# Triangular inverse of the scan in 32x32 blocks, with the last doubling as one off-diagonal block

## The chip, the cores and the metric

The kernel runs on one core of one Trainium2 chip. The metric is the device time of one execution in microseconds; the time to compare with is the median of three runs of the kernel before.

## What is computed

One inference step of a hybrid trunk layer. The input projection feeds two kinds of heads: attention heads, and eight RWKV-7 heads of width 64 whose state runs over time in both directions. Then come an output projection and routed experts. The change touches the RWKV part alone:

```
def rwkv_scan(r, decay, k, v, kk, a, s0, reverse):
    def step(s, inp):
        r_t, w_t, k_t, v_t, kk_t, a_t = inp
        sa = jnp.einsum('bhvk,bhk->bhv', s, -kk_t)
        s = (s * w_t[:, :, None, :] + sa[..., None] * (kk_t * a_t)[:, :, None, :]
             + v_t[..., None] * k_t[:, :, None, :])
        return s, jnp.einsum('bhvk,bhk->bhv', s, r_t)
```

There are 1152 tokens: 1024 of the sample and 128 of the prompt.

## The kernel before

The stages follow one another with a barrier between them: `head` (conditioning, norm, constant masks), `rwkv`, `attention`, `output`, `topk`, `experts`, `final`.

`rwkv` does not run the recurrence token by token. Time is cut into chunks of `CH` = 64 tokens, 18 in all. Within a chunk the recurrence is a linear system with a unit triangular 64x64 matrix I + L, so a chunk needs W = (I + L)^-1, some products of 64x64 matrices, and one state handed from chunk to chunk. Heads are taken in four pairs (`p`). The two heads of a pair lie in partitions 0 to 63 and 64 to 127 (`HS`), and both directions (`d`) are worked at once. Two chunks (`i`) make a group (`g`), so a pair has 9 groups and the kernel 36. All matmuls of a group are f32; TensorE runs each as two passes, and each pass has a weight load of its own, so a matmul of the code is two MATMUL and two LDWEIGHTS records.

What a group of the code does, with the names that the text uses:

- `M_products` (L652) multiplies B and KB by Q and R of a chunk. DVE's `masked` (L1178) multiplies the 64x128 results by the triangle masks `causal` and stores them in `M`.
- `inverse_start`: DVE builds the first W from the 2x2 blocks (L1186, L1192). PE multiplies it by the identity to get its transpose T (L700), and ACT copies T into `TW` (L950).
- Five doublings, `LV` = 5. Each has `level_X` (PE, L712: M by T), `level` (DVE, L1198: mask into X), `level_Y` (PE, L723 and L727: the updates of T and of W) and `added` (DVE, L1210: add to `TW`). The last doubling leaves T out. With 64x64 blocks all of them use full 64x64 products; the mask `level` picks the blocks that count.
- The state chain of the group before runs between these: `state_Z` (L737, and L746, L751 for the output), `state_U` (L762, W by Z), `state_S` (L772, L778). Each of two chunks needs Z, U and S in turn, with DVE (L1219, L1229, L1244) and ACT (L955, L960, L961) steps between.
- `tok_major` (L672) and `PV_KV` (L685, L688) prepare products for the group's own state chain.

The order in which these stand on PE, ACT and DVE is written out by hand in a loop over `g` on each engine; the engines meet by semaphores. PE takes its instructions in order, so an instruction that waits holds all behind it. At the end of a pair stands `finish`, and the projections of the next pair follow.

Of the kernel before, what the change touches and what calls it, by code (L numbers as in the profile page):

```python
# [26 lines left out]
P = 128  # L27
# [6 lines left out]
CH = 64  # L34
CHUNKS = NT // CH
# [85 lines left out]
def head(K, A):  # L121
# [8 lines left out]
    with ctx:  # L130
# [33 lines left out]
        with nc.Block() as block:  # L164
# [96 lines left out]
            def _(dve):  # L261
# [50 lines left out]
                for h in range(2):  # L312
                    hs = slice(h * CH, (h + 1) * CH)
                    V.tensor_copy(K.idc[hs, :], K.ident[hs, hs])
                    V.tensor_copy(K.causal[hs, :, :, :], tri[hs, :, :, hs])
                for lev in range(6):
                    link(V.tensor_scalar(cmp[:, :], xorf[:, :], float(2 ** (lev + 1)), None, ALU.is_lt))
                    link(V.scalar_tensor_tensor(cmp[:, :], xorf[:, :], float(2 ** lev), cmp[:, :], ALU.is_ge, ALU.mult))
                    for d in range(2):
                        for h in range(2):  # L320
                            hs = slice(h * CH, (h + 1) * CH)
                            last = V.scalar_tensor_tensor(K.level[hs, d, lev, :], cmp[hs, hs], -1.0, low[hs, d, hs],
                                                          ALU.mult, ALU.mult)
# [43 lines left out]
def rwkv(K, A):  # L367
# [10 lines left out]
    LV = 5  # L378
# [6 lines left out]
    with ctx:  # L385
# [26 lines left out]
        TW = [sb(f"TW{i}", [P, 2, 2, 2, CH]) for i in range(2)]  # L412
        X = sb("X", [P, 2, 2, CH])
        N0 = sb("N0", [P, 2, 2, CH])
# [5 lines left out]
        HS = [slice(h * HN, (h + 1) * HN) for h in range(2)]  # L420
        bank = K.bank
# [33 lines left out]
        t0ps, t0_ok, tw_ok = sem("T0_psum"), sem("T0_ok"), sem("TW_ok")  # L455
        xps, x_ok, yps = sem("X_psum"), sem("X_ok"), sem("TW_psum")
        zps, z_ok, ups, u_ok = sem("Z_psum"), sem("Z_ok"), sem("U_psum"), sem("U_ok")
# [13 lines left out]
        with nc.Block() as block:  # L471
# [55 lines left out]
            def _(pe):  # L527
# [69 lines left out]
                for p in range(PAIRS):  # L597
# [95 lines left out]
                    def inverse_start(g):  # L693
                        pe.wait_ge(w0_ok, p * GR + g + 1)
                        for d in range(2):
                            if g:
                                pe.wait_ge(tw_ok, p * (GR * NTW) + g * NTW - 1 + d)
                            for i in range(2):
                                for hs in HS:
# [1669 lines left out]
```

## Time and profile before

| | us |
|---|---|
| median of three runs (3862.14 to 3871.79) | 3862.87 |
| the profiled execution's own time | 3860.96 |
| its span | 3859.2 |
| one group of the scan in its steady part | 15.0 |
| groups | 36 |
| granted TensorE clock, mean of the span | 0.967 |

The span runs from the first to the last instruction of the profiled execution; the execution's own time has under 2 us around it. PE is TensorE's matmul record, PEld its weight load, DVE VectorE, ACT ScalarE. A matmul's record is longer than the time for which it keeps the array from the next one, since matmuls are pipelined; a row that merges n of them shows the time from the first's start to the last's end, and the spacing is read from that.

### The profile page before, as it was taken

Reading aid. Unit: us, or ns where it says so; the run is one execution under the profiler, and the core shown is the slowest. Engines: PE = TensorE matmul, PEld = TensorE weight load, DVE = VectorE, ACT = ScalarE, POOL = GpSimd, SP = SyncE. Lnnn points to the kernel's source line nnn. Section 1 sums busy time; section 2 is a strip of 40 time slices with the busy share of each in tenths; the row PEclk is TensorE's granted clock in tenths of the full one; section 3 lists DMA queues with packets and bytes.
Section 4 is the critical chain, followed back from the end, with each engine's and each line's share of the span. In section 5 each row is a group of like instructions: output and inputs, shape, how many; then the busy total and the mean of one; then the engine's idle time right before and its main releaser. Section 6 shows DMA issues by size and latency. Waiting matters only on the chain. (4 is left out here: it accounts for less than half of the span.)

```text
span 3859.2 us, 81746 instructions
## 1 busy us (share of the span) xinstructions
PE 3562.1 (92%) x37038; PEld 3101.1 (80%) x37038; DVE 1231.4 (32%) x3103; ACT 671.1 (17%) x1677; POOL 192.0 (5%) x150
## 2 busy tenths in 40 slices
PE   5899899999899979289999999999999999999995
PEld 2387685959555545189999999999999999999995
DVE  3376767777444443701111111111111111111112
ACT  2323324242144532100000000000000000000001
POOL 0010101010000000000000000000000000000000
PEclk7899999999999999589999999999999999999997
DMA  7200000000121022098887878788787878878773
GB/s 323 61 16 10 15 5 20 4 19 4 27 79 31 18 72 94 21 354 292 274 266 263 267 259 273 261 273 268 265 267 258 273 262 269 268 268 269 258 251 110
DMA packets 498393, 664.38 MB, mean 172 GB/s; under 512 B 31183, under 2 KB 437095, under 8 KB 494975
## 3 DMA queue, kind: packets, MB, share of 16 engines
q1 hardware_dynamic: 492238, 640.23, 49.5%
q0 software_dynamic: 5632, 18.88, 1.9%
q8 instruction: 291, 4.77, 0.5%
q14 instruction: 56, 0.45, 0.0%
q10 hardware_dynamic: 176, 0.05, 0.0%
HBM read 630.70 MB, written 28.36 MB: 171 GB/s over the span
## 5 line engine op out<-in xcount | busy, mean ns | idle before, releaser
L2094 PE MATMUL bank<-e_hid,e_wd 128*128 128x144 f32 x5632 | 760.1, 288 | 0.0
L2082 PE MATMUL bank<-e_xT,e_wg 128*128 128x144 f32 x5632 | 749.5, 286 | 1.0 <-ACT e_xT L2136 1.0
L2082 PE MATMUL bank<-e_xT,e_wu 128*128 128x144 f32 x5632 | 748.1, 286 | 0.0
L2082 PEld LDWEIGHTS bank<-e_xT,e_wg 128*128 128x128 f32 x5632 | 715.5, 190 | 1.0 <-issue 1.0
L2094 PEld LDWEIGHTS bank<-e_hid,e_wd 128*128 128x128 f32 x5632 | 710.5, 190 | 5.6
L2082 PEld LDWEIGHTS bank<-e_xT,e_wu 128*128 128x128 f32 x5632 | 714.4, 190 | 0.0
L2179 DVE TENSOR_TENSOR e_tm<-bank,e_sg 128x144 f32<-128x144 f32 x352 | 108.3, 308 | 1853.0 <-ACT e_sg L2143 1853.0
L2143 ACT ACTIVATE e_sg<-bank 128x144 f32<-128x144 f32 x352 | 102.2, 290 | 1998.4 <-PE bank L2082 1998.4
L532 PE MATMUL bank<-hT_x,wblk 128*128 128x512 f32 (+1 forms) x672 | 237.5, 511 | 14.5 <-DMA wblk<-in_w_in 8.5
L532 PEld LDWEIGHTS bank<-hT_x,wblk 128*128 128x128 f32 x672 | 114.1, 197 | 130.4 <-issue 112.4
L727 PE MATMUL bank<-r_TW,r_X 64*64 64x64 f32 x2880 | 167.5, 220 | 4.3 <-DVE r_X L1198 1.3
L1210 DVE TENSOR_TENSOR r_TW<-r_TW,bank 128x256 f32<-128x256 f32 (+1 forms) x360 | 135.4, 392 | 36.8 <-PE bank L727 33.0
L723 PE MATMUL bank<-r_X,r_TW 64*64 64x64 f32 x2304 | 142.1, 218 | 2.7 <-DVE r_X L1198 2.7
L727 PEld LDWEIGHTS bank<-r_TW,r_X 64*64 64x64 f32 x2880 | 136.2, 135 | 9.3 <-DVE r_X L1198 9.3
L1462 PE MATMUL bank<-hT_x,wblk 128*128 128x512 f32 (+1 forms) x384 | 138.7, 500 | 4.5 <-PEq L89 4.5
L712 PE MATMUL bank<-r_TW,r_M 64*64 64x64 f32 x2880 | 127.4, 223 | 5.7
L1198 DVE TENSOR_TENSOR r_X<-bank,level 128x128 f32<-128x128 f32 x360 | 96.6, 290 | 83.2 <-PE bank L712 79.7
L723 PEld LDWEIGHTS bank<-r_X,r_TW 64*64 64x64 f32 x2304 | 116.7, 135 | 4.1 <-DVE r_X L1198 3.8
L712 PEld LDWEIGHTS bank<-r_TW,r_M 64*64 64x64 f32 x2880 | 103.4, 134 | 16.7 <-ACT r_TW L950 9.7
L2182 DVE TENSOR_TENSOR e_hid<-bank,e_tm 128x144 f32<-128x144 f32 x352 | 108.2, 307 | 12.2
L1462 PEld LDWEIGHTS bank<-hT_x,wblk 128*128 128x128 f32 x384 | 62.6, 193 | 52.1 <-issue 50.6
L2049 POOL DMA_INDIRECT scratch_ffn<-e_ye,idx x16 | 25.8, 1610 | 1298.6 <-DVE e_ye L2198 1298.6
(324 smaller groups left out, 3469.9 us busy)
## 6 DMA issues: line engine op xcount, KB each, us to landing
e_wg<-in_e_gate SPq DMA_DIRECT2D x176, 1024.0 KB, 5.5
e_wu<-in_e_up SPq DMA_DIRECT2D x176, 1024.0 KB, 8.1
e_wd<-in_e_down SPq DMA_DIRECT2D x176, 1024.0 KB, 11.0
h_wmod<-in_w_mod SPq DMA_DIRECT2D x24, 1024.0 KB, 17.1
wblk<-in_w_in SPq DMA_DIRECT2D x22, 512.0 KB
h_x<-in_x_sample SPq DMA_DIRECT2D x8, 512.0 KB, 6.6
wo<-in_w_out SPq DMA_DIRECT2D x2, 2048.0 KB, 11.6
o_x<-in_x_sample SPq DMA_DIRECT2D x8, 512.0 KB, 4.2
```

What stands on the lines that cost most here:

```text
L532: last = nc.tensor.matmul(bank[first + c][:, 0:n], wblk[buf][:, kc, :], K.hT[:, kc, at:at + n], start=(kc == 0), stop=(kc == KD - 1))
L712: last = nc.tensor.matmul(bank[2 + d][hs, i * CH:(i + 1) * CH], M[g % 3][hs, d, i, 0, 0:CH], TW[g % 2][hs, d, 0, i, :], start=True, stop=True)
L723: nc.tensor.matmul(bank[4 + d][hs, i * CH:(i + 1) * CH], TW[g % 2][hs, d, 1, i, :], X[hs, d, i, :], start=True, stop=True)
L727: last = nc.tensor.matmul(bank[4 + d][hs, P + i * CH:P + (i + 1) * CH], X[hs, d, i, :], TW[g % 2][hs, d, 1, i, :], start=True, stop=True)
L1198: V.tensor_tensor(X[:, d, :, :], bank[2 + d][:, 0:P].rearrange("p (i t) -> p i t", t=CH), K.level[:, d, lev, :].unsqueeze(1).broadcast_to( ...
L1210: V.tensor_tensor(TW[g % 2][:, d, a:2, :, :].rearrange("p a i t -> p (a i t)"), TW[g % 2][:, d, a:2, :, :].rearrange("p a i t -> p (a i t) ...
L1462: last = nc.tensor.matmul(piece_bank(p, n)[:, 0:m], wblk[b][:, kc, :], K.hT[:, kc, at:at + m], start=(kc == 0), stop=(kc == KD - 1))
L2082: last = nc.tensor.matmul(bank[6 + b % 2][:, j * TOK:(j + 1) * TOK], w[s][:, k, f], xT[e % 2][:, k, :], start=(k == 0), stop=(k == KD - 1))
L2094: last = nc.tensor.matmul(bank[k // PER_BANK][:, c:c + TOK], wd[s][:, b % DUO, k * P:(k + 1) * P], hid[:, b % 2, :], start=(b == 0 and k % ...
L2143: nc.scalar.activation(sg[b % 2][:, :], bank[6 + b % 2][:, 0:TOK], ACT.Sigmoid).then_inc(sg_ok, 1)
L2179: V.tensor_tensor(tm[b % 2][:, :], bank[6 + b % 2][:, 0:TOK], sg[b % 2][:, :], ALU.mult)\
L2182: V.tensor_tensor(hid[:, b % 2, :], bank[6 + b % 2][:, TOK:2 * TOK], tm[b % 2][:, :], ALU.mult)\
```

## The change

The inverse is doubled only up to 32x32 blocks: `LV` falls from 5 to 4, and `X`, `N0`, `TW`, `level` hold 32 columns instead of 64 and use each partition quarter (`QS`) for its own diagonal block. `M_products` writes the parts of B by Q as 32x32 tiles, so that each quarter of the partitions finds its diagonal block in columns 0 to 31 and its off-diagonal block in columns 32 to 63; R and KB keep their shapes. The first T of a group comes from DVE's block transpose; PE's product with the identity and ACT's two copies are gone. The last doubling is one off-diagonal block per chunk, direction and head: `last_X` and `last_Y` on PE with an ACT copy between, and ACT puts the 64x64 inverse together in `WF` by eight activations on 32 partitions. `last_X` and `last_Y` of a group stand in the next group's code. `PV_KV` moves ahead of the fourth `level_X`.

```
-    LV = 5
+    LV = 4
...
                     def M_products(g, d):
                         for i in range(2):
-                            at = piece(d, 2 * g + i)
-                            for q, src in enumerate((B[d], KB[d])):
-                                for hs in HS:
-                                    last = nc.tensor.matmul(bank[d][hs, (2 * i + q) * P:(2 * i + q + 1) * P],
-                                                            src[hs, at], QR[d][hs, :, at], start=True, stop=True)
+                            at, c = piece(d, 2 * g + i), 2 * i * P
+                            for h, hs in enumerate(HS):
+                                for b in range(2):
+                                    rows = QS[2 * h + b]
+                                    own, other = at.start + b * HB, at.start + (1 - b) * HB
+                                    nc.tensor.matmul(bank[d][rows, c:c + HB], B[d][hs, own:own + HB],
+                                                     Q[d][hs, own:own + HB], start=True, stop=True)
+                                    nc.tensor.matmul(bank[d][rows, c + HB:c + CH], B[d][hs, own:own + HB],
+                                                     Q[d][hs, other:other + HB], start=True, stop=True)
+                            for hs in HS:
+                                nc.tensor.matmul(bank[d][hs, c + CH:c + P], B[d][hs, at], R[d][hs, at],
+                                                 start=True, stop=True)
+                            for hs in HS:
+                                last = nc.tensor.matmul(bank[d][hs, c + P:c + 2 * P], KB[d][hs, at], QR[d][hs, :, at],
+                                                        start=True, stop=True)
...
                             for i in range(2):
-                                for hs in HS:
-                                    last = nc.tensor.matmul(bank[2 + d][hs, i * CH:(i + 1) * CH],
-                                                            M[g % 3][hs, d, i, 0, 0:CH], TW[g % 2][hs, d, 0, i, :],
+                                for qs in QS:
+                                    last = nc.tensor.matmul(bank[2 + d][qs, i * HB:(i + 1) * HB],
+                                                            M[g % 3][qs, d, i, 0, 0:HB], TW[g % 2][qs, d, 0, i, :],
                                                             start=True, stop=True)
...
+                    def last_X(g):
+
+                        pe.wait_ge(tw_ok, p * (GR * NTW) + (g + 1) * NTW)
+                        for i in range(2):
+                            for d in range(2):
+                                for h in range(2):
+                                    src, to = QS[2 * h + d], QS[2 * h + 1 - d]
+                                    last = nc.tensor.matmul(bank[2][to, i * HB:(i + 1) * HB],
+                                                            M[g % 3][src, d, i, 0, HB:CH], TW[g % 2][src, d, 0, i, :],
+                                                            start=True, stop=True)
+                        last.then_inc(xlps, 1)
...
+                    def last_X(g):
+                        act.wait_ge(xlps, p * GR + g + 1)
+                        nc.scalar.activation(XL[:, :, :].rearrange("p i t -> p (i t)"), bank[2][:, 0:CH], ACT.Copy,
+                                             scale=-1.0).then_inc(xl_ok, 1)
+                        for q, qs in enumerate(QS):
+                            b = q % 2
+                            nc.scalar.activation(WF[g % 2][qs, :, :, b * HB:(b + 1) * HB], TW[g % 2][qs, :, 1, :, :], ACT.Copy)
+
+                    def last_Y(g):
+                        act.wait_ge(ylps, p * GR + g + 1)
+                        for q, qs in enumerate(QS):
+                            d = q % 2
+                            last = nc.scalar.activation(WF[g % 2][qs, d, :, (1 - d) * HB:(2 - d) * HB],
+                                                        bank[5][qs, CH:P].rearrange("p (i t) -> p i t", t=HB), ACT.Copy)
+                        last.then_inc(wf_ok, 1)
...
+                        dve.wait_ge(w0_ok, p * GR + g + 1)
+                        for d in range(2):
+                            V.transpose(TW[g % 2][:, d, 0, :, :].rearrange("p i t -> p (i t)"),
+                                        TW[g % 2][:, d, 1, :, :].rearrange("p i t -> p (i t)")).then_inc(t0_ok, 1)
```

`level_Y` changes as `level_X` does (four quarters instead of two halves), and `state_U` reads `WF` instead of `TW`. The masks made in `head` are copied in more and smaller pieces.

PE's order from the end of one group to the start of the next. Names read output, then inputs; the shape is output partitions by columns. Before, the group ends with `PV_KV`, the fifth doubling (L712, L727), the next group's T (L700) and its first `level_X`:

```order
L685 MATMUL bank<-r_vtok,r_M 64x64 x2
L688 MATMUL bank<-r_vtok,r_tok 64x64 x2
L712 MATMUL bank<-r_TW,r_M 64x64 x8
L727 MATMUL bank<-r_TW,r_X 64x64 x8
L700 MATMUL bank<-idc,r_TW 64x64 x8
L712 MATMUL bank<-r_TW,r_M 64x64 x8
L737 MATMUL bank<-r_S,r_QR 64x64 x4
L746 MATMUL bank<-r_QR,r_S 64x64 x4
L751 MATMUL bank<-r_M,r_vtok 64x64 x4
L652 MATMUL bank<-r_QR,r_B 64x128 x2
L652 MATMUL bank<-r_QR,r_K 64x128 x2
```

The same place in the changed kernel, where L722 is `level_X`, L732 and L735 `level_Y`, L747 `last_X`, and L665, L667, L670, L673 `M_products`:

```order
L709 MATMUL bank<-r_vtok,r_tok 64x64 x2
L722 MATMUL bank<-r_TW,r_M 32x32 x16
L732 MATMUL bank<-r_X,r_TW 32x32 x4
L735 MATMUL bank<-r_TW,r_X 32x32 x4
...
L747 MATMUL bank<-r_TW,r_M 32x32 x8
L768 MATMUL bank<-r_S,r_QR 64x64 x4
L777 MATMUL bank<-r_QR,r_S 64x64 x4
L782 MATMUL bank<-r_M,r_vtok 64x64 x4
L665 MATMUL bank<-r_QR,r_B 32x32
L667 MATMUL bank<-r_QR,r_B 32x32
...
L670 MATMUL bank<-r_QR,r_B 64x64 x2
L673 MATMUL bank<-r_QR,r_K 64x128 x2
```

The small tiles now alternate with the 64-wide ones, and nothing stands between the fourth `level_Y` and `last_X`.

DVE at the end of a steady group before: the fourth `level`, the state step, the next group's first W, then two rounds of `added` with a `level` between:

```order
L1198 TENSOR_TENSOR r_X<-bank,level 128x128 x2
L1244 SCALAR_TENSOR_TENSOR r_S<-bank,r_e,r_SK 128x64 x2
L1186 TENSOR_TENSOR r_N<-r_M,level 128x128 x2
L1192 TENSOR_TENSOR r_TW<-r_N,idc 128x128 x2
L1210 TENSOR_TENSOR r_TW<-r_TW,bank 128x256 x2
L1198 TENSOR_TENSOR r_X<-bank,level 128x128 x2
L1210 TENSOR_TENSOR r_TW<-r_TW,bank 128x128 x2
```

And in the changed kernel:

```order
L1248 TENSOR_TENSOR r_X<-bank,level 128x64 x2
L1293 SCALAR_TENSOR_TENSOR r_S<-bank,r_e,r_SK 128x64 x2
L1231 TENSOR_TENSOR r_N<-r_M,level 128x64 x2
L1238 TENSOR_TENSOR r_TW<-r_N,id 128x64 x2
L1242 STREAM_TRANSPOSE r_TW<-r_TW 128x64 x2
L1259 TENSOR_TENSOR r_TW<-r_TW,bank 128x128 x2
```

The two block transposes stand ahead of the fourth `added`, for which `last_X` waits.

## Rows read from the trace of the kernel before

**Rows 1.** The page: busy time, and granted clock and busy tenths in 40 slices.

```profile
PE 3562.1 (92%) x37038; PEld 3101.1 (80%) x37038; DVE 1231.4 (32%) x3103; ACT 671.1 (17%) x1677; POOL 192.0 (5%) x150
PEclk7899999999999999589999999999999999999997
```

**Rows 2.** Timeline: L700 opening group 1 and group 8 of the first pair.

```profile
231.21 0.68 PE L700 MATMUL bank<-idc,r_TW 64*64 64x64 f32 x16 [0.25 <-DVE r_TW L1210]
...
336.19 0.68 PE L700 MATMUL bank<-idc,r_TW 64*64 64x64 f32 x16 [0.20 <-DVE r_TW L1210]
```

**Rows 3.** Timeline: the group's end, each matmul row with its merged count.

```profile
334.47 0.68 PE L712 MATMUL bank<-r_TW,r_M 64*64 64x64 f32 x16
335.26 0.73 PE L727 MATMUL bank<-r_TW,r_X 64*64 64x64 f32 x16
337.00 0.27 PE L712 MATMUL bank<-r_TW,r_M 64*64 64x64 f32 x2
```

**Rows 4.** Timeline: unbroken streams of 64 and of 128 columns.

```profile
214.85 2.31 PE L660 MATMUL bank<-idc,r_v 64*64 64x64 f32 x72 [2.60 <-DVE r_v L1038]
323.22 0.39 PE L652 MATMUL bank<-r_QR,r_B 64*64 64x128 f32 x4
323.44 0.38 PE L652 MATMUL bank<-r_QR,r_K 64*64 64x128 f32 x4
```

**Rows 5.** Timeline: four column tiles at once (L352), one full array (L1807), both 512 columns.

```profile
38.63 2.33 PE L352 MATMUL bank<-h_wmod,h_cond 128*32 128x512 f32 x20
1554.65 1.88 PE L1807 MATMUL bank<-wo,yB 128*128 128x512 f32 x4
```

**Rows 6.** One line each: record durations of loads and matmuls, min/median/max ns.

```profile
L352 PEld LDWEIGHTS bank<-h_wmod,h_cond x192: 106/110/156, 36.0 to 80.1; 128*32 128x32 f32 x192
L723 PEld LDWEIGHTS bank<-r_X,r_TW x2304: 129/135/135, 219.7 to 997.6; 64*64 64x64 f32 x192
L723 PE MATMUL bank<-r_X,r_TW x2304: 216/218/267, 219.8 to 997.7; 64*64 64x64 f32 x192
L652 PE MATMUL bank<-r_QR,r_B x576: 269/269/320, 210.3 to 976.7; 64*64 64x128 f32 x192
```

**Rows 7.** Timeline of PE where the tile shape changes (rows*columns of the array).

```profile
1004.66 0.40 PE L778 MATMUL bank<-r_M,r_U 64*64 64x64 f32 x8
1005.41 0.45 PE L576 MATMUL bank<-idc,r_S 64*64 64x64 f32 x8 [0.35 <-DVE r_S L1244]
1005.79 2.21 PE L546 MATMUL bank<-r_aa,head_ones 128*128 128x512 f32 x6
...
1121.26 0.44 PE L1549 MATMUL bank<-t_pt,t_vtok 64*64 64x128 f32 x4
1121.63 1.13 PE L1503 MATMUL bank<-t_k,t_q 64*128 64x512 f32 x4
```

**Rows 8.** DVE's groups from 200 to 1010 us, shapes apart: busy us, mean ns.

```profile
L1210 DVE TENSOR_TENSOR r_TW<-r_TW,bank 128x256 f32<-128x256 f32 x288 | 115.1, 418 | 26.7 <-PE bank L727 23.1
L1198 DVE TENSOR_TENSOR r_X<-bank,level 128x128 f32<-128x128 f32 x360 | 96.6, 290 | 83.2 <-PE bank L712 79.7
L1102 DVE TENSOR_TENSOR r_mid<-r_t 128x18 f32<-128x18 f32 x3 | 0.6, 190 | 0.1
```

**Rows 9.** Timeline of DVE: pairs of instructions, x2 merged.

```profile
332.58 0.48 DVE L1244 SCALAR_TENSOR_TENSOR r_S<-bank,r_e,r_SK 128x64 f32<-128x64 f32 x2
332.98 0.48 DVE L1186 TENSOR_TENSOR r_N<-r_M,level 128x128 f32<-128x128 f32 x2
333.49 0.49 DVE L1192 TENSOR_TENSOR r_TW<-r_N,idc 128x128 f32<-128x128 f32 x2
```

**Rows 10.** Timeline: a pair's last group, and ACT's copies in the scan.

```profile
1000.05 0.52 DVE L1210 TENSOR_TENSOR r_TW<-r_TW,bank 128x128 f32<-128x128 f32 x2 [0.32 <-PE bank L727]
1000.87 0.45 PE L762 MATMUL bank<-r_Z,r_TW 64*64 64x64 f32 x8
...
L960 ACT ACTIVATE r_t<-bank 128x64 f32<-128x64 f32 x72 | 16.1, 223 | 60.6 <-PE bank L778 60.6
```

More of the change, by code:

```diff
@@ L319, in _ @@
                     for d in range(2):
-                        for h in range(2):
-                            hs = slice(h * CH, (h + 1) * CH)
-                            last = V.scalar_tensor_tensor(K.level[hs, d, lev, :], cmp[hs, hs], -1.0, low[hs, d, hs],
+                        for q in range(4):
+                            here = slice(q * HB, (q + 1) * HB)
+                            last = V.scalar_tensor_tensor(K.level[here, d, lev, :], cmp[here, here], -1.0, low[here, d, here],
                                                           ALU.mult, ALU.mult)
@@ L420, in rwkv @@
         HS = [slice(h * HN, (h + 1) * HN) for h in range(2)]
+        QS = [slice(q * HB, (q + 1) * HB) for q in range(4)]
         bank = K.bank
@@ L691, in PV_KV @@
                         last.then_inc(kvps, 1)
[L693 to L698, printed above, removed]
-                                for hs in HS:
-                                    last = nc.tensor.matmul(bank[4 + d][hs, i * CH:(i + 1) * CH], TW[g % 2][hs, d, 1, i, :],
-                                                            K.idc[hs, :], start=True, stop=True)
-                            last.then_inc(t0ps, 1)
                     def level_X(g, lev):
@@ new lines, in last_Y @@
+                    def last_Y(g):
+                        pe.wait_ge(xl_ok, p * GR + g + 1)
+                        for i in range(2):
+                            for d in range(2):
+                                for h in range(2):
+                                    src, to = QS[2 * h + 1 - d], QS[2 * h + d]
+                                    last = nc.tensor.matmul(bank[5][to, CH + i * HB:CH + (i + 1) * HB], XL[src, i, :],
+                                                            TW[g % 2][src, d, 1, i, :], start=True, stop=True)
+                        last.then_inc(ylps, 1)
@@ L789, in _ @@
                         j = 2 * (g - 1)
-                        if g < GR:
-                            inverse_start(g)
-                            level_X(g, 1)
                         if g:
+                            last_X(g - 1)
                             state_Z(j)
@@ L800, in _ @@
                             M_products(g + 1, 0)
+                        if g:
+                            last_Y(g - 1)
                         if g < GR:
-                            level_Y(g, 1)
+                            level_X(g, 1)
                         if g + 1 < GR:
@@ L830, in _ @@
                             level_Y(g, 4)
-                            PV_KV(g)
-                            level_X(g, 5)
-                            level_Y(g, 5)
                 finish_first(PAIRS - 1)
@@ L1262, in _ @@
                         if g < GR:
-                            added(g, 1)
+                            level(g, 1)
                         if g + 1 < GR:
@@ L1284, in _ @@
                             added(g, 4)
-                            level(g, 5)
-                            added(g, 5)
                         if g == 0:
```

97 lines of the change are left out of this document (54 added, 43 removed).

## The prediction

> **What bounds the kernel now.** The page first [rows 1]: TensorE is at work nearly all the time, and the scan, in which every changed line but the masks in `head` stands, lies in the slices with the high VectorE digits, where the granted clock reads 9, that is, its higher level of 2.4 GHz. The experts behind it are untouched.
>
> Then the timeline of one group. L700 opens group 1 of the first pair at 231.21 and group 8 at 336.19 [rows 2]: seven groups in 104.98 us, 15.0 each. What is PE's own share of that? The rows give the spacing of a stream: 72 passes of 64 columns take 2.31 us, of which about 0.22 is the last one's record, so 2.09/71 = 29.4 ns a pass; with 128 columns the next four start 0.22 later, 54.5 a pass [rows 4]. A matmul of the code is two passes, so 58.5 and 109 ns. By the code a steady group before has 200 matmuls of 64 columns (`inverse_start` 8, the doublings 112, the state chain 48, `tok_major` and `PV_KV` 32) and 16 of 128: 11.7 + 1.7 = 13.4 us. The other 1.6 us are waits, most of them at the group's end: L712 streams 0.47 us from 334.47 and L727 starts 0.79 after it, L700 0.93 after that, and L712 0.81 after L700 [rows 2, 3], together 1.1 us of waiting. So the group is bound by TensorE's stream, with a latency tail at its end.
>
> **The change, part by part.** All times are per steady group.
>
> *Matmuls.* Now 88 of 64 columns (the 80 outside inverse and `M_products`, and R 8), 8 of 128 (KB), 32 with 64 rows and 32 columns of the array (B by Q), and 208 in 32x32 tiles (`level_X` 64, `level_Y` 128, `last_X` and `last_Y` 16). The wide ones cost 88 x 58.5 + 8 x 109 = 6.0 us.
>
> What a 32x32 one costs no row of the scan shows. Two facts bear on it. A record gets 51 ns longer from 64 to 128 columns [rows 6], 0.8 ns a column, and a load from 32 to 64 gets 25 longer; so 32 columns keep their own tile busy 27 ns, and with the 4 to 5 ns that the 64-wide pairs have over their columns (58.5 against 53) about 32 ns. And tiles run side by side: the 64-wide pair does (58.5 ns for two passes of which each streams 53), and in L352 four tiles do, at 512 columns: 20 passes in 2.33 us less one record of 0.59 are five sets of four, spaced 0.43 us, the spacing of one single full-array pass of L1807 ((1.88 - 0.59)/3) [rows 5]. If four 32x32 tiles behave so, a set of four passes costs 32 ns and a matmul 16: 208 x 16 = 3.3 us. Bounds: 28 ns a set, if only the columns count (2.9 us), and no gain over 64-wide, 29.2 a pass (12.1 us). I take 3.3, by the row with four tiles.
>
> In B by Q the two neighbours share a tile and can't overlap. Each matmul costs 32 ns if it overlaps the next one on another tile, 64 if none does: 1.0 to 2.0 us; I take 1.5.
>
> *Changes of tile shape.* This is the part that the diff doesn't show. After the last of the eight L576 (64*64) starts, at 1005.41 + 0.45 - 0.22 = 1005.64, L546 (128*128) starts 0.15 later, where a 64-wide stream goes on after 0.054: 0.095 lost. L1549 (64*64) to L1503 (64*128) costs the same: last start 1121.26 + 0.44 - 0.27 = 1121.43, next 0.20 later, against 0.103 in the stream: 0.097. So rows or columns alike, a change of shape lets the array run empty. The first load after an empty array is exposed too: eight passes of L576 take 0.45, eight of L778 in the stream 0.40 [rows 7]. A change then costs 0.095 + 0.05 = 0.145 into 64-wide and 0.095 + 0.025 = 0.12 into 32-wide. Before, the whole group is 64*64 and pays none. Now, through the loop: `last_X` | `state_Z` | B by Q | R, KB | B by Q | R, KB | `last_Y`, `level_X` 1 | B by Q | R, KB | B by Q | R, KB | `level_Y` 1 | U | X2 | S | Y2 | `tok_major` | X3 | Z | Y3 | U, `PV_KV` | X4 | S | Y4: 23 changes, 11 into 64-wide and 12 into 32-wide, 1.6 + 1.4 = 3.0 us.
>
> PE's stream is then 6.0 + 3.3 + 1.5 + 3.0 = 13.8 us, against 13.4 before: what the smaller tiles save, the changes of shape take.
>
> *Waits.* The old tail goes: fifth doubling, L700, ACT's two copies. A new one takes its place. `last_X` needs the fourth `added`, and nothing stands on PE between it and the fourth `level_Y`; behind it are `state_Z` and `M_products`. DVE from the start of its state step: L1244 0.40, L1186 0.51, L1192 0.41, two `added` of 128 columns 0.52 [rows 9, 10]. With 64 columns instead of 128 a DVE step is shorter by about 0.055 (0.19 at 18 columns, 0.29 at 128 [rows 8]), and L1192's pair now has a wait of 0.1 after it as L1186's has: 0.40 + 0.39 + 0.39. The two block transposes have no row: no less than 0.3 as two plain 64-column steps, no more than 0.8 as two of 0.42 like L1210's wide form [rows 8]; I take 0.5. Sum 0.40 + 0.39 + 0.39 + 0.5 + 0.52 = 2.2, and 0.23 of latency on both sides; PE meanwhile does half of `state_S` 0.23, a change 0.12, and `level_Y` 4 0.51. PE waits 1.6 us. At the first doubling DVE has `masked` (0.69, as now) ahead of `added`; PE's U and two changes nearly cover it, 0.2 is left. Together 1.8, against 1.6 before.
>
> *ACT.* L950's two copies leave; the XL copy and eight pieces of WF come. A step of 64 columns takes ACT 0.22 [rows 10], one of 128 I put 0.055 higher by DVE's slope; that is some 2.2 us. They lie beside `state_Z` and both `M_products` on PE, over 5 us, so in the steady part they cost nothing. Without that cover they are on the path: in each pair's last group `state_U` starts 0.3 us after `added` ends (1000.57 to 1000.87 [rows 10]), and now waits for `last_X` 0.33, XL 0.25, four copies 1.0, four more 0.85: 2.4. That is 2.1 more, four times, 8 us.
>
> *Masks in `head`*: some 25 more small DVE instructions of about 0.1 us while `head` waits for its weights; nothing.
>
> *Sum.* A group becomes 13.8 + 1.8 = 15.6 us, 0.6 more. 32 of the 36 groups follow another one in their pair: 19 us; a pair's first group I leave as it is. With the 8 of the tails 27. The profiled execution took 3860.96 (its span 1.8 less) and lies 1.9 under the median; so 3861 + 27 and 2: **3890 us**. With the low ends (2.9, 1.0, transposes 0.3) a group is 14.5 and the time 3855; with the high ends of B by Q and the transposes 16.4 and 3916.
>
> **Rivals.**
>
> *Small tiles are no cheaper than 64-wide ones.* A pass may have a floor of its own, a load and a matmul each 29 ns, whatever its columns; no row of the scan has fewer than 64. For it: the unbroken streams of the scan never go below 29 ns a pass [rows 4]. Against it: the 20 passes of L352 take 1.74 to the last start, four set spacings of 0.43 and 0.02 for the three gaps in a set, so four tiles start 7 ns apart. If the floor holds, 240 matmuls cost 14.0 instead of 4.8 us, and the waits shrink by 1.5 since `level_Y` 4 covers more: 7.7 above the 15.6, 8.3 above now, 32 times and 8: about 4137. Chance 0.18. If two tiles overlap but not four, 208 matmuls cost 6.6 instead of 3.3, the waits shrink by 0.5, and a group takes 18.4: about 3980. Chance 0.10.
>
> The Trainium skill, "TensorE: Matmul & The Clock Gate", section "Wait — 56ns, not 53.3ns?", says that matmuls never start less than about 25 ns apart, however few columns they have. By that floor, taken for each of the 480 small passes, they would cost 12.0 us, and the time would be some 4075 us, an estimate from that page. The trace does not settle it: sets of four tiles start closer than that, but only at 512 columns.
>
> *The change of shape is free among small tiles* (the side of faster). The rows show it into 64*128 and into 128*128, not between 64*64 and 32*32. If it costs nothing there, PE's stream is 10.8, the waits stay, and a group takes 12.6: 32 x -2.4 + 8, about 3795. It decides from about 0.09 us a change down, the exposed load included, where I have 0.13: there 32 groups win back the tails. Against it: both shown changes, of rows and of columns, cost the same 0.095, which looks like the array running empty and not like a matter of size. 0.10.
>
> *The group's time is not PE's.* If the state chain set the 15.0, nothing would move but the tails, 3871. Against it: 13.4 of 15.0 are PE's stream. 0.04.
>
> **How the numbers follow.** The forecast case has 0.58, the floor 0.18, the half overlap 0.10, the free change 0.10, no movement 0.04. The time is that of the first, 3890. What a measurement of this kernel tells from no change is about 0.3%, 12 us. Faster by more than that (below 3851): the free change and a sliver of the first case, 0.13. Within it: the low part of the first case and no movement, 0.17. Slower 0.70. For eight in ten the range has to reach into the floor's case: 3852 to 4110.
>
> **What would show it.** Right: in the new trace `level_X` of sixteen matmuls spans about 0.45 us with its last record, and 32x32 records start four to a set; between L722 and a 64-wide neighbour a gap of some 0.15; PE idle for DVE's r_TW about 1.6 us ahead of L747; groups 15.6 apart. Wrong: `level_Y` passes spaced 25 ns or more (the floor), gaps at changes of shape under 0.1, a transpose of DVE over 0.5 each, or ACT's WF copies ending after `M_products`, so that the first `level_Y` waits for them. A granted clock that falls to 1.2 GHz in the scan would make it slower than any case here.

## The result and the profile after

The changed kernel takes 4040.51 us (median of four runs, 4031.74 to 4042.03) against 3863.11; the ratio is 1.0449, interval 1.0428 to 1.0471. The profiled execution spans 4040.0 us. The forecast was 3890: the side was right, but the loss is 177 us and not 27.

From the page of the changed kernel (busy time; TensorE's granted clock over the span; PE's instruction queue; three costly groups, with the idle time ahead of them and its releaser):

```profile
span 4040.0 us, 99196 instructions
PE 3630.3 (90%) x45678; PEld 3094.3 (77%) x45678; DVE 1152.1 (29%) x3061; ACT 732.9 (18%) x1929; POOL 191.9 (5%) x150
PEclk7898988889879999968999999999999999999997
q8 instruction: 359, 5.88, 0.6%
...
L732 PE MATMUL bank<-r_X,r_TW 32*32 32x32 f32 x4608 | 116.0, 204 | 28.3 <-issue 23.9
L735 PE MATMUL bank<-r_TW,r_X 32*32 32x32 f32 x4608 | 113.6, 201 | 26.6 <-issue 26.4
L722 PE MATMUL bank<-r_TW,r_M 32*32 32x32 f32 x4608 | 80.0, 205 | 16.4 <-issue 14.5
```

Two things here were in no term of the forecast. PE stands still ahead of the doublings' matmuls, and the releaser is "issue": no semaphore, no tile, nothing that the profile shows. And the granted clock reads 7 or 8 in several slices of the scan (slices 3 to 12), where it read 9 [rows 1].

The timeline of PE through part of one group (start, length, work; idle time before it in brackets; rows between are left out at the dots):

```profile
319.81 0.22 PE L735 MATMUL bank<-r_TW,r_X 32*32 32x32 f32 x2 [0.67 <-issue]
...
320.26 0.45 PE L793 MATMUL bank<-r_Z,r_WF 64*64 64x64 f32 x8
320.64 0.45 PE L722 MATMUL bank<-r_TW,r_M 32*32 32x32 f32 x32
321.08 0.45 PE L803 MATMUL bank<-r_U,r_tok 64*64 64x64 f32 x8
321.37 0.40 PE L809 MATMUL bank<-r_M,r_U 64*64 64x64 f32 x8
321.69 0.26 PE L732 MATMUL bank<-r_X,r_TW 32*32 32x32 f32 x8
321.78 0.24 PE L735 MATMUL bank<-r_TW,r_X 32*32 32x32 f32 x8
321.84 0.24 PE L732 MATMUL bank<-r_X,r_TW 32*32 32x32 f32 x8
321.91 0.24 PE L735 MATMUL bank<-r_TW,r_X 32*32 32x32 f32 x8
321.97 0.22 PE L732 MATMUL bank<-r_X,r_TW 32*32 32x32 f32 x3
323.48 0.22 PE L732 MATMUL bank<-r_X,r_TW 32*32 32x32 f32 x3 [1.29 <-issue]
...
327.21 0.22 PE L735 MATMUL bank<-r_TW,r_X 32*32 32x32 f32 x3 [0.74 <-issue]
...
330.79 0.38 PE L803 MATMUL bank<-r_U,r_tok 64*64 64x64 f32 x5 [0.98 <-issue]
...
333.18 0.44 PE L747 MATMUL bank<-r_TW,r_M 32*32 32x32 f32 x16 [1.09 <-DVE r_TW L1259]
```

What the forecast priced is there at its price. `level_X`'s 32 passes of L722 span 0.45 us, 8.1 ns a pass. From the last start of L793 (320.26 + 0.45 - 0.22) to L722 are 0.15. But the burst at 321.97 breaks off after three of eight passes and goes on 1.29 us late, again at 327.21 and at 330.79, the last time in the middle of 64-wide work: the stops don't belong to a line or a tile shape. From one resumption to the next (319.81, 323.48, 327.21, 330.79) it is 3.6 to 3.7 us.

The windows of six steady groups, before and then after (length, busy time and records by engine, granted clock, DMA), each with the row of the instruction queue in the DMA view of the same stretch (packets, MB, share):

```profile
243.70:333.70 90.00, 87.25 (x2600) 83.85 (x2596) 64.63 (x218) 21.23 (x84) 0.00 (x0) 1.00 0.02 4
```

```profile
q8 instruction: 21, 0.34, 1.6%
```

```profile
249.50:369.80 120.30, 97.93 (x4040) 81.83 (x4036) 50.61 (x206) 32.01 (x127) 0.00 (x0) 0.86 0.02 5
```

```profile
q8 instruction: 32, 0.52, 1.8%
```

A packet is 16 KB. Before, PE issued 866 matmul and load records in a group of 15.0 us, 247 for each packet; after, 1346 in 20.1 us, 252 for each. Over the whole program the same row of the page reads, before:

```profile
q8 instruction: 291, 4.77, 0.5%
```

and 359 packets after, while PE's matmul and load records divided by 256 are 289 and 357. So nearly all packets are PE's, 256 instructions each, and in the steady groups the mean time from one to the next has gone from 4.3 to 3.8 us. Over all four pairs the 32 periods from one group to the next average 19.5 us, 14.8 before (from the starts of `PV_KV`): 151 us. The other 26 lie in the first groups and the tails of the pairs.

Five explanations are tried below. Theory **supply**: PE can't get its instructions faster than 256 in about 3.6 us, 14 ns each, and a load and matmul pair of 8 ns of array time is starved. Rivals: **array** (small passes are dear in themselves: the floor of the forecast's first rival), **clock** (PE is slow because it was granted the lower clock), **waits** (DVE and ACT around the new last doubling), **shape** (the changes of tile shape).

### The profile page after: what moved, and what is told of

It is laid out like the page before. It is cut to its first block and busy times, and to the rows that moved or that the text cites. A ratio compares the mean times of both kernels' runs of the same rounds, so it can differ in the third digit from the quotient of the medians.

```text
span 4040.0 us, 99196 instructions
## 1 busy us (share of the span) xinstructions
PE 3630.3 (90%) x45678; PEld 3094.3 (77%) x45678; DVE 1152.1 (29%) x3061; ACT 732.9 (18%) x1929; POOL 191.9 (5%) x150
## 5 line engine op out<-in xcount | busy, mean ns | idle before, releaser
L543 PE MATMUL bank<-hT_x,wblk 128*128 128x512 f32 (+1 forms) x672 | 237.7, 511 | 14.8 <-DMA wblk<-in_w_in 8.8
L732 PE MATMUL bank<-r_X,r_TW 32*32 32x32 f32 x4608 | 116.0, 204 | 28.3 <-issue 23.9
L735 PE MATMUL bank<-r_TW,r_X 32*32 32x32 f32 x4608 | 113.6, 201 | 26.6 <-issue 26.4
L732 PEld LDWEIGHTS bank<-r_X,r_TW 32*32 32x32 f32 x4608 | 93.4, 113 | 44.6 <-issue 31.6
L735 PEld LDWEIGHTS bank<-r_TW,r_X 32*32 32x32 f32 x4608 | 95.3, 115 | 30.5 <-issue 30.5
L1259 DVE TENSOR_TENSOR r_TW<-r_TW,bank 128x128 f32<-128x128 f32 x288 | 79.5, 283 | 87.0 <-PE bank L735 83.2
L1248 DVE TENSOR_TENSOR r_X<-bank,level 128x64 f32<-128x64 f32 x288 | 56.1, 223 | 152.4 <-PE bank L722 152.2
L722 PE MATMUL bank<-r_TW,r_M 32*32 32x32 f32 x4608 | 80.0, 205 | 16.4 <-issue 14.5
L722 PEld LDWEIGHTS bank<-r_TW,r_M 32*32 32x32 f32 x4608 | 60.8, 115 | 28.3 <-issue 17.6
```

The lines of the kernel that those rows point to most:

```text
L543: last = nc.tensor.matmul(bank[first + c][:, 0:n], wblk[buf][:, kc, :], K.hT[:, kc, at:at + n], start=(kc == 0), stop=(kc == KD - 1))
L722: last = nc.tensor.matmul(bank[2 + d][qs, i * HB:(i + 1) * HB], M[g % 3][qs, d, i, 0, 0:HB], TW[g % 2][qs, d, 0, i, :], start=True, stop=True)
L732: nc.tensor.matmul(bank[4 + d][qs, i * HB:(i + 1) * HB], TW[g % 2][qs, d, 1, i, :], X[qs, d, i, :], start=True, stop=True)
L735: last = nc.tensor.matmul(bank[4 + d][qs, CH + i * HB:CH + (i + 1) * HB], X[qs, d, i, :], TW[g % 2][qs, d, 1, i, :], start=True, stop=True)
L1248: V.tensor_tensor(X[:, d, :, :], bank[2 + d][:, 0:CH].rearrange("p (i t) -> p i t", t=HB), K.level[:, d, lev, :].unsqueeze(1).broadcast_to ...
L1259: V.tensor_tensor(TW[g % 2][:, d, :, :, :].rearrange("p a i t -> p (a i t)"), TW[g % 2][:, d, :, :, :].rearrange("p a i t -> p (a i t)"), ...
```

## Experiments

### Streams that wait for nothing

In the kernel before, ahead of the scan's first projections; `wide_run` issues 128x512 matmuls, `small_run(n, w, src)` n calls in w x w tiles along the diagonal, `idc` is f32 and `low16` bf16 (the results are read by nobody):

```
+                wide_run(8)
+                small_run(512, 32, K.idc)
+                wide_run(8)
+                small_run(512, 32, low16)
+                wide_run(8)
+                small_run(512, 64, K.idc)
+                wide_run(8)
+                for _ in range(16):
+                    small_run(16, 32, K.idc)
+                    small_run(8, 64, K.idc)
```

> The kernel before, with extra matmuls ahead of the first projections of the scan's stage: five streams on PE that wait for nothing and whose results nobody reads, each behind eight 128x512 matmuls: 512 calls of 32x32 on four diagonal tiles in f32 (1024 passes), the same in bf16 (512 passes), 512 calls of 64x64 in f32, and sixteen turns of 16 calls of 32x32 and 8 calls of 64x64. Supply theory (PE receives its instructions in packets of 256, and no faster than one packet in about 3.6 us, so a load and matmul pair can't come oftener than every 28 to 29 ns over a long stretch): the first f32 stream of 2048 instructions begins at about 8 ns a pass, stands still for 0.6 to 1.7 us after some 256 instructions of each kind of packet, and takes about 8 x 3.6 = 29 us; the bf16 stream of 1024 instructions takes some 12 to 14 us although it has half the passes; the 64x64 stream takes about 29 us too, unless its own pace of some 18 ns a pass is slower. Floor theory (each small pass costs 25 to 29 ns by itself): starts are evenly 25 to 29 ns apart from the first pass on, with no long stops. Array theory (passes at 8 ns, nothing else): 8 us for the first stream, no stops. Shape theory: only the last stream, with 31 changes, is slow, by about 31 x 0.14 = 4 us.

Measured (one run): the timeline of the f32 stream and the start of the bf16 one in 32x32 tiles, then of the one in 64x64.

```profile
99.05 1.75 PE L576 MATMUL bank<-idc 32*32 32x32 f32 x185
102.78 1.27 PE L576 MATMUL bank<-idc 32*32 32x32 f32 x128 [1.98 <-issue]
106.51 1.93 PE L576 MATMUL bank<-idc 32*32 32x32 f32 x128 [2.46 <-issue]
110.24 1.92 PE L576 MATMUL bank<-idc 32*32 32x32 f32 x128 [1.80 <-issue]
113.70 1.93 PE L576 MATMUL bank<-idc 32*32 32x32 f32 x128 [1.53 <-issue]
117.15 1.93 PE L576 MATMUL bank<-idc 32*32 32x32 f32 x128 [1.52 <-issue]
120.88 1.93 PE L576 MATMUL bank<-idc 32*32 32x32 f32 x128 [1.80 <-issue]
124.61 1.18 PE L576 MATMUL bank<-idc 32*32 32x32 f32 x71 [1.80 <-issue]
...
134.28 1.53 PE L576 MATMUL bank<-causal 32*32 32x32 bf16 x169
137.71 1.19 PE L576 MATMUL bank<-causal 32*32 32x32 bf16 x128 [1.91 <-issue]
141.17 1.22 PE L576 MATMUL bank<-causal 32*32 32x32 bf16 x128 [2.27 <-issue]
```

```profile
154.51 30.08 PE L576 MATMUL bank<-idc 64*64 64x64 f32 x1024
```

The instruction queue over the f32 stream in 32x32 tiles (99.0 to 125.7 us) and over the one in 64x64 (154.5 to 184.5):

```profile
q8 instruction: 7, 0.11, 1.8%
q8 instruction: 8, 0.13, 1.7%
```

PE runs 128 passes, 256 instructions, at full pace (1.27 less a record of 0.2: 8 ns a pass) and stands until the next 256 are there, every 3.45 to 3.73 us; over the six steps from 102.78 to 124.61, 3.64 us. One pass a matmul or two, bf16 or f32: the step is the same. Nor does the clock set it: from 106.5 to 125.7 us the granted clock is 0.50, the bursts last 1.93 instead of 1.27, and the steps are no longer. The 64x64 stream has as many instructions and no stop: its own 29 ns a pass take 3.75 us for 256. So 64-wide tiles were just at the point where supply and array balance, and anything quicker buys nothing. No pass costs 25 ns by itself: the array rival falls. The Trainium skill, "TensorE: Matmul & The Clock Gate", section "Wait — 56ns, not 53.3ns?", states that floor; across four tiles these rows show 8, and over a long stretch 28, for another reason. The Trainium skill, "Runtime: NRT & Kernel Launch", section "Instruction fetch mechanics", says that instructions come in blocks of 256 and that crossing a block is "mostly hidden". By these rows the first holds, and the second fails for a stream this dense.

The windows of the four streams (f32 32x32, bf16 32x32, f32 64x64, mixed) show something else, the granted clock, third figure from the right:

```profile
99.00:125.70 26.70, 13.81 (x1025) 12.82 (x1024) 0.00 (x0) 0.00 (x0) 0.00 (x0) 0.61 0.02 4
134.30:145.70 11.40, 4.72 (x513) 4.39 (x512) 0.00 (x0) 0.00 (x0) 0.00 (x0) 0.71 0.02 4
154.50:184.50 30.00, 30.00 (x1025) 29.94 (x1024) 0.00 (x0) 0.00 (x0) 0.00 (x0) 1.00 0.02 4
191.60:210.10 18.50, 16.75 (x769) 14.59 (x768) 0.00 (x0) 0.00 (x0) 0.00 (x0) 1.00 0.02 4
```

Streams of small passes with stops between them spend much of their time at the lower level, 1.2 GHz; the stream without stops and the mixed one, which has few, don't. So the clock is not a rival only; it may follow from the stops.

### Half the instructions of the doublings

```
-                      M[g % 3][qs, d, i, 0, 0:HB], TW[g % 2][qs, d, 0, i, :],
+                      D16[qs, :], D16[qs, :],
```

and so for both matmuls of `level_Y`; `D16` is a bf16 tile of zeros. This kernel leaves out the doublings' values.

> The changed kernel, with the operands of its four doublings' matmuls (X and both updates) taken from a bf16 tile of zeros: each call is one pass in place of two, so a group issues some 192 fewer loads and 192 fewer matmuls (about 960 instructions instead of 1344); waits, order and shapes of tiles stay. It leaves out the doublings' values. Supply theory: a group goes from 19.9 us to about 960 x 14.4 ns = 13.8, held at 14.5 to 15.5 by waits and shape changes: 3840 to 3880 us, and the stops without a releaser nearly vanish. Array theory (only the 8 ns of each pass counts): 192 x 8 ns = 1.5 us a group, 55 us in all: about 3985. Clock theory (the scan is slower because PE is granted the lower clock for long stretches): about 3985 too, unless the clock also comes back.

Measured 3850.24 us (one run). Windows of two of its groups:

```profile
262.00:275.40 13.40, 11.61 (x488) 9.66 (x486) 7.82 (x35) 5.21 (x21) 0.00 (x0) 1.00 0.01 4
303.20:320.00 16.80, 15.22 (x486) 12.49 (x484) 7.78 (x35) 5.21 (x21) 0.00 (x0) 0.70 0.01 4
```

974 instead of 1346 records, and a group at full clock is 13.4 us, where those of the changed kernel take 18.5 or more: 190 us gone for 55 us of array time. PE's idle time under "issue" in the scan falls from 101.8 us (119 entries) to 7.9 (18). That is supply's number. The second window is the clock's: the same records, granted 0.70, take 3.4 us more. With fewer instructions in the way, the lower clock shows in full.

### The kernel before with as many instructions

```
+                if d and lev < LV:
+                    for m in range(56):
+                        rows = slice(32 * (m % 4), 32 * (m % 4) + 32)
+                        nc.tensor.matmul(bank[5][rows, 3 * P:3 * P + 32], K.causal[rows, 0, 0, 0:32],
+                                         K.causal[rows, 0, 0, 0:32], start=True, stop=True)
```

> The kernel before, with 56 extra bf16 matmuls of 32x32 in each of the first four doublings (224 passes and 224 loads a group, 448 instructions, so that a group issues some 1350 as the changed kernel does), results read by nobody. Supply theory: groups of 19.3 to 19.9 us and stops without a releaser: 4000 to 4040 us. Array theory: 224 x 8 ns and eight shape changes of 0.13 us add 2.8 us a group at most: 3960 at most and no stops. If the small tiles of the changed kernel are slow for a reason of its order of work alone: 3865 to 3900.

Measured 4012.93 (one run), in the range of supply, though the groups, 18.9 us on average, are a little under its 19.3 to 19.9; the clock is that of before (0.967). The waits of the scan now have 30.5 us under "issue" in 71 entries where before had none. Array time and shape changes of the extra matmuls explain up to 3960; the other 50 us or more are left for supply, with none of the change's own parts and at full clock.

### Parts of the change alone

First T by the block transpose in the kernel before (PE's L700 and ACT's L950 gone, DVE's two transposes behind W):

> The kernel before, with one part of the change alone: the first T of each group by DVE's block transpose (two transposes of 128x128 behind W's start) in place of PE's 16 passes of L700 and ACT's two copies L950. 34 instructions fewer a group on PE, and PE's wait for W's start and for ACT's copy goes. Supply theory: PE of before already takes in some 900 instructions in 15.0 us, 256 in 4.3 us, so it is not bound by supply and gains what its own path gives: 0.3 us of passes and 0.3 to 0.6 us of waits a group, 20 to 30 us: 3833 to 3845. If the two transposes (some 0.4 us each by the 0.22 us of 128x64) land on DVE's path instead: no change, 3855 to 3870. The change's own T part as the cause of its loss would show as slower, above 3875.

Measured 3839.65, ratio 0.9936 (0.9919 to 0.9952): this part gains 24 us, 0.7 us a group.

Then the changed kernel's order, first T and off-diagonal last doubling, with 64x64 tiles for the four doublings and M's products as before:

> The changed kernel's order, its first T by DVE's block transpose and its last doubling as one off-diagonal block (32x32 tiles, ACT's copies), but M's products and the four doublings in 64x64 tiles as before. It issues as many instructions a group as the kernel before less the 32 of the first T. Supply theory: no packet comes late, groups of 14.0 to 14.6 us, 3830 to 3865. If the off-diagonal block's two further round trips through ACT and the moved order are what costs (waits), groups stay above 16 us: 3920 or more. Against the run with the first T alone (3840) this shows what the last doubling as one block is worth by itself: 32 passes go from 29 to 8 ns each (-0.7 us a group) and four to six shape changes of some 0.13 us come (+0.5 to +0.8 us), so within 10 us of it if nothing waits.

Measured 3854.95, ratio 0.9975 (0.9965 to 0.9985): inside the expected range, but 15 us behind the first T alone, and the timeline shows on what (this version also needs only half of ACT's copies into the inverse, since `state_U` reads `TW` again):

```profile
317.56 0.28 PE L721 MATMUL bank<-r_TW,r_X 64*64 64x64 f32 x4
319.35 0.33 PE L733 MATMUL bank<-r_TW,r_M 32*32 32x32 f32 x16 [1.51 <-DVE r_TW L1241]
```

That is the wait ahead of `last_X` which the prediction put at 1.6 us.

And the changed kernel with M's products wide again, so that only the doublings are in small tiles (DVE has one more operation a group, which folds the 64-wide N into 32 columns):

```
-                                    rows = QS[2 * h + b]
...
+                                    last = nc.tensor.matmul(bank[d][hs, (2 * i + q) * P:(2 * i + q + 1) * P],
+                                                            src[hs, at], QR[d][hs, :, at], start=True, stop=True)
```

> The changed kernel with the products of M as before: B by QR in 64x64 tiles with 128 columns (8 calls a group in place of 40 small and middling ones), the doublings pick their 32x32 blocks out of it, and DVE folds the 64-wide N into 32 columns with one more operation. 64 passes fewer a group, so 128 instructions fewer of some 1350, and no change of tile shape inside M's products. Supply theory: half a packet of 3.7 us less in a group of 19.5 us: 17.7 us, 60 to 70 us in all, 3970 to 3985. Array theory: the 64 extra passes at 13.5 ns and eight shape changes go (1.9 us) and 8 calls of 128 columns are dearer by some 0.9 us: 1.0 us a group, 4005. If waits for DVE were what holds the groups, the added DVE operation makes it slower than the changed kernel: above 4040.

Measured 3976.92 (3971.25 to 3982.6), groups of 18.0 us. That is within supply's range; array's number (4005) and waits' (over 4040) are missed. 128 instructions fewer at 14.2 ns are 1.8 us a group, and 65 us in 36 groups.

So the small tiles of the doublings, with ACT's other copies and DVE's added operation, cost 122 us (3855 to 3977), those of B by Q 64 (3977 to 4040), the last doubling as one block, with its order, costs 15, and the first T gives 24.

### Is it the waits, or the order?

`state_Z` ahead of `last_X` in the changed kernel, and then this together with `PV_KV` behind the fourth doubling, first with 64x64 tiles and then in the changed kernel itself (ACT's copies of `PV_KV` move behind `state_Y` with it):

```
-                            last_X(g - 1)
                             state_Z(j)
+                            last_X(g - 1)
...
-                            PV_KV(g)
                             level_X(g, 4)
...
                             level_Y(g, 4)
+                            PV_KV(g)
```

> The changed kernel with state_Z's matmuls put ahead of last_X's on PE, so that 0.6 us of work covers PE's wait for DVE's last added T and W (23.8 us in 36 times in the changed kernel). Wait theory: about 0.6 x 36 = 20 us come back: 4020. Supply theory: the time that PE stands for DVE is time in which instructions arrive, so cutting the wait only brings the next stop forward: 4035 to 4042, no difference that can be told.

> The run with the off-diagonal last doubling and 64x64 tiles elsewhere (3855), with two moves: PV_KV's matmuls back behind the fourth doubling (and its ACT copies behind state_Y), and state_Z's ahead of last_X's, so that 1.0 + 0.7 us of PE's work covers the 1.5 us for which last_X waits for DVE in each group there. Wait theory for that run: 1.2 to 1.5 us a group come back where nothing else is late: 3800 to 3815, and then the whole change without its small tiles beats both kernels. If supply held that run already (256 instructions in 4.6 us there, far from 3.6), nothing would come: 3850. If the copies of PV and KV on ACT now hold XL's copy, half comes back: 3830.

> The changed kernel with the same two moves that took 32 us off the version with 64x64 tiles (PV_KV's matmuls behind the fourth doubling, state_Z's ahead of last_X's). Supply theory: PE stands for DVE less, and for instructions as much more; 5.1 to 5.3 packets a group at 3.6 us stay: 4010 to 4040, less than half of what the moves gave there. Wait theory: the 24 to 32 us come off here too: 4008 or less, groups of 18.6. What the lower clock costs (some 0.9 us a group by the run with 64 columns) may move by 10 us either way with how the stops fall.

| | with 64x64 tiles | changed kernel |
|---|---|---|
| as it was | 3854.95 | 4040.51 |
| Z first | | 4025.15 (ratio 1.042, 1.039 to 1.0451) |
| both moves | 3822.95 (ratio 0.9889, 0.9871 to 0.9906) | 4040.24 (ratio 1.0449, 1.0432 to 1.0467) |

The same two moves are worth 32 us where instructions come in time and nothing where they don't. With 64x64 tiles that is between the two numbers of the expectation (3800 to 3815 for the waits, 3830 if half came back): the periods from group to group fell from 14.5 to 13.25 us on average, 41 us in all, and 9 us were lost again outside them, which was not followed. In the changed kernel the time is at the upper end of supply's range (4010 to 4040), and the waits under "issue" grow from 101.8 us (119 entries) to 129.5 (137): what DVE no longer holds, supply does. Z first by itself came out 15 us lower, between both theories' numbers and nearer to that of the waits (4020), with the granted clock at 0.949 against 0.942; its interval overlaps that of the changed kernel, so that run tells nothing apart.

With both moves and 64x64 tiles every steady group is 13.36 us, and its window shows PE without a gap (and the queue's row):

```profile
242.80:323.00 80.20, 80.09 (x2504) 76.63 (x2499) 61.15 (x206) 24.05 (x102) 0.00 (x0) 1.00 0.02 4
```

```profile
q8 instruction: 20, 0.33, 1.7%
```

834 records a group, a packet every 4.0 us. This version beats both kernels: some 41 us under before, 218 under the change.

### More array time, the same instructions

```
-                  M[g % 3][qs, d, i, 0, 0:HB], TW[g % 2][qs, d, 0, i, :],
+                  M[g % 3][qs, d, i, 0, 0:HB],
+                  TW[g % 2][qs, d, 0, i, :].unsqueeze(1).broadcast_to([HB, 2, HB]),
```

and so for both matmuls of `level_Y`; DVE reads only the first copy.

> The changed kernel, with every matmul of the four doublings moving its 32 columns twice (64 columns, the second copy into PSUM columns that nobody reads): the same number of instructions, tiles, waits and shape changes, but more array time in 384 passes a group. Array theory (the changed kernel is slow because its small passes take PE's time): 384 x 8 ns = 3 us a group more, 4150. Supply theory: the passes have room while the next packet is awaited, so most of it is hidden: 4040 to 4060. Clock theory (the small, short passes make PE lose its full clock, and that is what costs): longer passes keep the engine fuller, the clock comes back to about 0.97 and the time falls below 4000.

Measured 4007.97, ratio 1.0372 (1.0349 to 1.0395), and the window of six of its groups, with the queue's row:

```profile
248.30:361.20 112.90, 99.93 (x4042) 83.53 (x4040) 51.64 (x206) 32.02 (x127) 0.00 (x0) 1.00 0.02 5
```

```profile
q8 instruction: 31, 0.51, 1.7%
```

All three numbers were missed: the 110 us of the array theory don't come, and the time even falls by 32, though not below 4000. PE does more work on the same 8082 records, is granted its full clock (1.00, 0.963 over the span, against 0.86 and 0.942), and a packet comes every 3.6 us. Array time was free, as supply says. How much the lower clock cost the changed kernel beside it, this run bounds only roughly, since it changes both at once. The changed kernel's own six groups of the window above:

```profile
249.50:269.00 19.50, 15.68 (x680) 13.27 (x676) 9.53 (x36) 5.33 (x21) 0.00 (x0) 0.91 0.03 6
269.00:287.70 18.70, 14.57 (x679) 12.16 (x676) 8.11 (x35) 5.33 (x21) 0.00 (x0) 1.00 0.02 4
287.70:309.70 22.00, 17.93 (x680) 14.89 (x678) 8.27 (x35) 5.21 (x21) 0.00 (x0) 0.77 0.01 4
309.70:328.20 18.50, 14.55 (x680) 12.23 (x677) 8.39 (x34) 5.21 (x21) 0.00 (x0) 1.00 0.02 5
328.20:348.40 20.20, 17.54 (x678) 14.58 (x676) 8.12 (x35) 5.32 (x21) 0.00 (x0) 0.75 0.02 5
348.40:369.80 21.40, 17.67 (x680) 14.70 (x677) 8.18 (x35) 5.60 (x22) 0.00 (x0) 0.76 0.02 4
```

The two at 1.00 are the short ones here, but not everywhere. Of the 28 periods from one group to the next in the four pairs (the last of each pair has fewer matmuls), 11 were granted 1.00 throughout: they take 18.5 to 20.7 us, 19.3 on average. The 14 with a granted clock under 0.9 take 19.2 to 22.0, 20.4 on average. All 28 average 19.9, so by the changed kernel's own groups the lower clock costs 0.6 us a group, some 16 us in all; the 32 us of the run with 64 columns are the upper figure.

Records a group, the time of 256 of them, and the clock, from the windows of each kernel:

| kernel | records a group | us for 256 | clock there | us |
|---|---|---|---|---|
| before | 866 | 4.4 | 1.00 | 3863.11 |
| 64x64 tiles, both moves | 834 | 4.1 | 1.00 | 3822.95 |
| before and 56 more a doubling | 1312 | 3.7 | 1.00 | 4012.93 |
| changed, wide M | 1212 | 3.8 | 0.96 | 3976.92 |
| changed | 1346 | 3.8 | 0.86 | 4040.51 |
| changed, 64 columns | 1347 | 3.6 | 1.00 | 4007.97 |
| the 32x32 f32 stream | | 3.64 | 0.61 | |

## Why the prediction was wrong

Point by point, by the prediction's steps:

- **What bounds the kernel now.** Right: PE's stream. But the 29.4 ns a pass of its 64-wide stream [rows 4], which it read as array time, was also within a nanosecond of what supply allows. The rows of before could not show that second limit, since nothing in the scan ran faster.
- **Matmuls.** Sets of four 32x32 passes cost 32 ns, as taken from the row with four tiles. B by Q came cheaper than 1.5: in the changed kernel's timeline eight of its matmuls, 16 passes, start from 317.93 to 318.09 us, and the next shape follows at 318.21; so the 32 matmuls take about 0.7 us, 1.1 with the changes of shape behind them.
- **Changes of tile shape.** Right in kind and size: 0.15 from L793 to L722. In the mixed stream a turn of 32 small and 16 wide passes takes 0.995 us where no stop falls into it (the first one ends its wide passes at 192.437 us, the next at 193.432), of which the passes are 32 x 8 + 16 x 29.4 ns = 0.73, so both directions together cost 0.27, the forecast's 0.145 + 0.12.
- **The step that failed** is the sentence "PE's stream is then 6.0 + 3.3 + 1.5 + 3.0 = 13.8 us". It priced the stream by the array alone. The same stream has 1346 records, and 1346 x 14.2 ns (3.64 us for 256) are 19.1 us; by the shortest and the longest step of the stream, 3.45 and 3.73, 18.1 to 19.6. A group's stream is at least the larger of the two, and the groups measured at full clock are 19.3 on average. For the kernel before the same product is 12.3, under its 15.0. Splitting a 64x64 matmul into 32x32 ones gave back array time and paid in instructions, the dearer of the two.
- **Waits.** The wait ahead of `last_X` is 1.51 us in the version with 64x64 tiles, where 1.6 was forecast; in the changed kernel it is 0.7 on average (23.8 us in 36 times) presumably since the stops let DVE catch up. The transposes took 224 ns each, 0.45 for the two against 0.5. ACT's WF copies cost nothing in the steady part; in the pairs' last groups `state_U` waits for them 4.9 us in four times and the first `level_Y` 2.7 us in three, together about the 8 us forecast for the tails. The forecast had named that wait of `level_Y` as a sign of being wrong; it came only where no `M_products` cover the copies.
- **The granted clock** was named as what would make it slower than any case; it did fall, to 0.86 in the six groups shown, and cost some 16 to 32 us. The time is still under that of the slowest case (4137).
- **The rivals.** All of them had the wrong mechanism. Small tiles are not as dear as 64-wide ones (4137, and 4075 by the floor that the Trainium skill, "TensorE: Matmul & The Clock Gate", states in "Wait — 56ns, not 53.3ns?"), and it is four tiles that overlap, not two (3980): a pass in a burst costs 8 ns. Shape changes were not free, and the group's time was PE's.
- **Luck.** The measured time lies within the range of 3852 to 4110, but only because the range had been stretched toward the floor's case, whose mechanism is not there. That a long stretch of small passes costs 28 ns each by supply, close to that case's 29, is a coincidence. The side, slower, came from terms that make 27 us of the 177.

In size: the 32 periods from group to group cost 151 us, where the forecast had 0.6 us in each, 19. Of the 132 us that it didn't have, 16 to 32 are the lower clock's by the two estimates above, and the remaining 100 to 116 are put down to supply. The last 26 of the 177 lie in the first groups and the tails of the pairs, where the forecast had 8; they were not taken apart.

What stays open: what exactly makes the clock fall in the scan. The stops and the lower clock came together in the streams and in the changed kernel, but 56 more matmuls a doubling brought stops (30.5 us) without it, and the run with 64 columns kept its stops (57.6 us under "issue") and lost the low clock. The lower clock was seen where short passes and stops came together; nothing separates the two further. Open too is why single groups at full clock differ by up to 2 us, and what sets the step of 3.6 us. Nor was it tried whether a looped program would be supplied differently.

## What to carry to other kernels

Count a stream's instructions beside its array time: for PE the larger of (array time) and (records x 14 ns) is the least that it costs, and an f32 matmul brings four records, a bf16 one two. Over a long stretch a pass cost no less than some 28 ns here, 32x32 in f32 and in bf16 and 64x64 alike; what gains there is fewer passes: larger calls, fewer of them, or one pass (bf16) in place of two where the values allow it. Idle time with the releaser "issue" in the middle of a burst, at equal steps of time whatever the line, is the sign.

A change of several parts is worth taking apart: here the first T by DVE, the off-diagonal last doubling and two moves together make the kernel 1.1% faster, and the small tiles, put on top of that, make it 4.5% slower.

## What the hardware showed that was not expected

- PE's instructions come 256 at a time, no oftener than every 3.45 to 3.73 us in an unbroken stream; the stops last 1.5 to 2.5 us there and up to 1.8 in the scan. A lower granted clock (0.50) leaves the steps as they are.
- More array work made a kernel faster: 64 columns in place of 32 in 384 passes a group took 32 us off (4040.51 to 4007.97), with the granted clock up from 0.942 to 0.963.
- 32x32 passes on four diagonal tiles start 8 ns apart on average in f32 and in bf16; 64x64 ones on two tiles 29 ns.
